# Rotary's swapped rows in the first block: twelve SBUF to SBUF DMAs per layer in place of sixteen permutation products

## The chip, the cores and the metric

One core of a Trainium2 chip runs the whole program in one launch. Its engines have a queue each: PE (TensorE, matrix products into PSUM, which has 8 banks), DVE (VectorE), ACT (ScalarE), POOL (GpSimd), and SP, which here only issues DMAs. They run beside each other and meet at semaphores. The metric is the time of one execution on the device in microseconds (us).

## The reference, cut to what matters

Two blocks of two layers each on 512 tokens of width 1024. The change is in the first block, in the rotary step of both of its layers. Of one layer:

```
h = x @ w_in[l]
c_q, c_kv, k_r, gate_a, q_d, k_d, v_d, gate_b, gates = split(h)
q_a = (rms_norm(c_q, g_q) @ w_q_up).reshape(8 heads, 64 + 32)
q_a = concat(q_a[..., :64], rotary(q_a[..., 64:], 32))
kv  = (rms_norm(c_kv, g_kv) @ w_kv_up)          # 8 heads, 64 (keys) + 64 (values)
k_a = concat(kv[..., :64], rotary(k_r, 32) for every head)
q_b, k_b = rotary(q_d, 16), rotary(k_d, 16)     # 4 heads x 2 halves of 64, first 16 of each
o_a = attention(q_a, k_a, v_a); o_b = differential_attention(q_b, k_b, v_d, lambda)
... gates, two branch products, merge, w_out, layer norm

rotary: x1, x2 = xr[:half], xr[half:]
        out = concat(x1 * cos - x2 * sin, x2 * cos + x1 * sin)
```

The second block (modulation, two feed-forward parts, a state space mixer) is not touched. It needs a vector `mod = silu(c) @ mod_w`, 9216 columns per layer, and the first block computes that beside its own work.

## The kernel before

Activations lie turned: channels on the 128 partitions, 512 tokens along the row. Each fp32 weight block of 128 x 1024 is fetched by SP into one of four slots (`w_raw`, line 136), copied by ACT into a high part (`w_hi`, L144), and POOL makes the low part (`w_lo`, L152). PE then makes three products per 128 x 128 piece (L158 to L160). SP fetches block n only when `w_lo` of block n - 4 is done, ACT makes `w_hi` of n only when PE has used block n - 4.

Work stands in an order written out by hand, the same in both layers. By blocks of the ring: 0 to 3 the latents and the rope key; 4 to 7 `QD`; 8 to 11 `KD`; 12 and 13 the heads of `QT` (banks `qh`), 14 the keys of all heads (`kh`, into `KTr`), 15 the values (`VA`); 16 to 19 the values `VD` (`values`, L178 to L180, which first waits for all four of its banks, and these are the banks that ACT's copies of `VA` free); 20 to 23 gate a; then the attention, with the rest of the weights as filler.

Rotary: the rows of a half are needed at the places of the other half. PE does this with a permutation matrix that also carries the sign (`rot_a`, `rot_d`, in `tables_sb`), in fp32, one product per head: four for `QD` between the products of `KD` (`swap`, L605), four for `KD` behind block 12, four for the heads 0 to 3 of `QT` behind block 13, and four for heads 4 to 7 between the key products. The result stands in banks 4 to 7. DVE then does three operations per head (`rotate`, L1044 to L1047): swapped rows times the sine table into `tmp`, x times cosine, and the sum. Sixteen heads in that order, `s_rot` counts them. The rope key is done the same way with one more product of its own (L616).

Behind the sixteen rotations, DVE works through `mod_w` in chunks of 128 x 1024 (`chunk`, L1086 and L1088, two operations each); 20 of them stand between the rotations and the attention, in groups of four. A group's four chunks add up in one of two sums (`macc_a`), and PE turns each sum by eight small products (`mod_turn`, L599), the first of them behind the third block of `VD`. A chunk is loaded by SP into one of five slots (L507). The first three chunks (0, 1, 2) stand in SP's queue at block 18, the next behind the fetch of block 24.

ACT's order there: copies of `QD`, `KD`, the rope key into all heads, `QT` heads 0 to 3, `w_hi` of 16, `QT` heads 4 to 7, `w_hi` of 17, eight copies of `KTr`, four of `VA`, `w_hi` of 18 and 19, and then `w_hi` of 20, which waits for the first block of `VD`.

## Time and profile before

| | us |
|---|---|
| median of 3 runs | 3594.82 |
| lowest, highest | 3591.64, 3597.8 |
| the profiled execution, own time | 3595.13 |
| its span in the trace | 3593.3 |
| PE busy | 3365.8 (94%) |
| PE weight load busy | 2630.1 (73%) |
| DVE busy | 2024.1 (56%) |
| ACT busy | 1170.8 (33%) |
| POOL busy | 1336.6 (37%) |

The span is what the trace covers; 1.83 us of the execution's own time lie around it. A product of 128 x 512 shows as about 0.39 us long, yet the next one starts 0.23 us after it: the ends are modelled and overlap, so PE's real pace is read from the starts. Busy shares are means over the whole program, while the change lies in two stretches of some 90 us, about 80 to 190 us and 622 to 732 us into the span. Where an engine stood idle, the row says in brackets for how long and what ended the wait.

### The profile page before, as it was taken

To read this page: it belongs to the slowest core of one execution; us is meant where nothing else is said; L and a number is where in the kernel's file an instruction comes from. 1 tells how busy PE (TensorE), PEld (TensorE's weight loads), DVE (VectorE), ACT (ScalarE), POOL (GpSimd) and SP (SyncE) were. 2 spreads that over 40 slices of the span, in tenths; PEclk is the share of its full clock that TensorE was granted. 3 is DMA by queue.
4 is the path that set the end of the run, shared out by engine and by line. 5 is a ranking of instruction groups with operands and counts; after the bars stand their busy time and mean duration, and the time that the engine had idled before them with its cause. 6 is when DMAs were issued, how large, how long until landed. Compare 5 with 4: busy or idle time off the path is not lost. (4 is left out here: it accounts for less than half of the span.)

```text
span 3593.3 us, 44542 instructions
## 1 busy us (share of the span) xinstructions
PE 3365.8 (94%) x16330; PEld 2630.1 (73%) x16330; DVE 2024.1 (56%) x2706; ACT 1170.8 (33%) x1792; POOL 1336.6 (37%) x565
## 2 busy tenths in 40 slices
PE   8999899999896999899998999969998999999997
PEld 6656677656675888787776888758887876778886
DVE  3876685876685444896274543154459944644412
ACT  3354323354323223333243222332233324332232
POOL 3302243302331445544043445534454521534453
PEclk9999999999997999999799999979999988999999
DMA  4513382513372332577123332233234951423321
GB/s 129 180 36 115 116 252 74 175 45 115 107 239 58 106 98 81 100 106 112 45 89 88 94 99 81 66 99 94 86 90 84 123 86 48 126 71 99 93 84 63
DMA packets 587729, 363.85 MB, mean 101 GB/s; under 512 B 57890, under 2 KB 537516, under 8 KB 587308
## 3 DMA queue, kind: packets, MB, share of 16 engines
q1 hardware_dynamic: 587188, 361.51, 38.7%
q8 instruction: 106, 1.74, 0.2%
q14 instruction: 59, 0.48, 0.0%
q10 hardware_dynamic: 376, 0.12, 0.0%
HBM read 346.63 MB, written 12.58 MB: 100 GB/s over the span
## 5 line engine op out<-in xcount | busy, mean ns | idle before, releaser
L152 POOL TENSOR_TENSOR w_lo<-w_raw,w_hi 128x1024 fp32r<-128x1024 f32 (+2 forms) x552 | 1328.6, 2412 | 2209.9 <-ACT w_hi L144 2209.6
L158 PE MATMUL bank<-xh,w_lo 128*128 128x512 f32 x2432 | 985.4, 405 | 61.2 <-DVE xl L2298 25.1
L160 PE MATMUL bank<-xh,w_hi 128*128 128x512 f32 x2432 | 971.8, 400 | 0.0
L159 PE MATMUL bank<-xl,w_hi 128*128 128x512 f32 x2432 | 971.2, 399 | 0.0
L144 ACT ACTIVATE w_hi<-w_raw 128x1024 fp32r<-128x1024 f32 (+2 forms) x552 | 564.8, 1027 | 787.4 <-PE bank L160 722.2
L158 PEld LDWEIGHTS bank<-xh,w_lo 128*128 128x128 f32 x2432 | 468.7, 193 | 185.6 <-issue 41.3
L159 PEld LDWEIGHTS bank<-xl,w_hi 128*128 128x128 f32 x2432 | 469.2, 193 | 106.0 <-issue 4.3
L160 PEld LDWEIGHTS bank<-xh,w_hi 128*128 128x128 f32 x2432 | 468.0, 192 | 101.4
L158 PE MATMUL bank<-HH,w_lo 128*128 128x512 f32 x704 | 278.6, 396 | 0.0
L160 PE MATMUL bank<-HH,w_hi 128*128 128x512 f32 x704 | 278.5, 396 | 0.0
L159 PE MATMUL bank<-HL,w_hi 128*128 128x512 f32 x704 | 278.4, 395 | 0.0
L2455 DVE SCALAR_TENSOR_TENSOR HL<-th,HH 128x512 f32 x88 | 244.0, 2773 | 10.9
L2451 DVE TENSOR_TENSOR th<-th,bank 128x512 f32<-128x512 f32 x88 | 60.5, 687 | 321.5 <-PE bank L160 320.4
L1088 DVE SCALAR_TENSOR_TENSOR macc_b_l<-m_raw_l,cs_l,macc_b_l 128x512 f32<-128x512 f32 x182 | 180.3, 991 | 6.9 <-DMA m_raw_l<-in_mod_w_dram 1.8
L2052 ACT ACTIVATE th<-bank 128x512 f32<-128x512 f32 x88 | 52.6, 598 | 392.9 <-PE bank L160 363.3
L2448 DVE SCALAR_TENSOR_TENSOR th<-th,bank 128x512 f32<-128x512 f32 x88 | 60.5, 687 | 180.2 <-ACT th L2052 180.2
L2271 DVE TENSOR_TENSOR tot_sq<-tot_sq,sqt 128x512 f32<-128x512 f32 x24 | 52.6, 2194 | 192.7 <-ACT sqt L2012 192.3
L158 PEld LDWEIGHTS bank<-HH,w_lo 128*128 128x128 f32 x704 | 132.2, 188 | 32.1
L160 PEld LDWEIGHTS bank<-HH,w_hi 128*128 128x128 f32 x704 | 132.2, 188 | 32.0
L159 PEld LDWEIGHTS bank<-HL,w_hi 128*128 128x128 f32 x704 | 132.2, 188 | 31.9
L2615 DVE TENSOR_REDUCE nm<-bank 128x1 f32<-128x128 f32 (+3 forms) x64 | 28.4, 486 | 175.3 <-PE bank L1916 175.3
L2260 DVE TENSOR_TENSOR ycr<-y,xT 128x512 f32<-128x512 f32 x30 | 31.3, 1045 | 126.5 <-ACT y L2009 126.2
(502 smaller groups left out, 4547.1 us busy)
## 6 DMA issues: line engine op xcount, KB each, us to landing
w_raw<-in_ffn_w_in_dram SPq DMA_DIRECT2D x176, 512.0 KB, 3.8
m_raw_l<-in_mod_w_dram SPq DMA_DIRECT2D x144, 512.0 KB, 5.1
w_raw<-in_w_in_dram SPq DMA_DIRECT2D x80, 512.0 KB, 4.0
w_raw<-in_mix_w_in_dram SPq DMA_DIRECT2D x64, 512.0 KB, 9.2
w_raw<-in_ffn_w_out_dram SPq DMA_DIRECT2D x64, 384.0 KB, 3.5
w_raw<-in_ffn_w_out_dram SPq DMA_DIRECT2D x64, 320.0 KB, 3.2
w_raw<-in_w_out_dram SPq DMA_DIRECT2D x16, 512.0 KB, 4.7
w_raw<-in_glu_w_dram SPq DMA_DIRECT2D x32, 256.0 KB, 3.1
```

What stands on the lines that cost most here:

```text
L144: nc.scalar.activation(ring.hi[s][:, 0:width], ring.raw[s][:, 0:width], ACT.Copy).then_inc(ring.hi_done, 1)
L152: nc.gpsimd.tensor_tensor(ring.lo[s][:, 0:width], ring.raw[s][:, 0:width], ring.hi[s][:, 0:width].bitcast(F32), ALU.subtract).then_inc(rin ...
L158: nc.tensor.matmul(out, wl, xh, start=start, stop=False)
L159: nc.tensor.matmul(out, wh, xl, start=False, stop=False)
L160: return nc.tensor.matmul(out, wh, xh, start=False, stop=stop)
L1088: ins = V.scalar_tensor_tensor(macc[:, :], w, cc, macc[:, :], ALU.mult, ALU.add)
L2052: nc.scalar.activation(th[v][:, :], bank[2 * v], ACT.Tanh, scale=0.5).then_inc(s["tanh"], 1)
L2260: V.tensor_tensor(to[:, :], y[:, m, :], xT[:, m, :], MUL).then_inc(s["y_cross"], 1)
L2271: V.tensor_tensor(tot["sq"][:, :], tot["sq"][:, :], sqt[m % 2][:, :], ADD).then_inc(s["y_added"], 1)
L2448: V.scalar_tensor_tensor(t[:, :], t[:, :], 1.0, bank[2 * v], ADD, MUL).then_inc(evac[2 * v], 1)
L2451: V.tensor_tensor(t[:, :], t[:, :], bank[2 * v + 1], MUL).then_inc(evac[2 * v + 1], 1)
L2455: V.scalar_tensor_tensor(HL[:, to, :], t[:, None, :], 0.5, HH[:, to, :].bitcast(F32), MUL, SUB).then_inc(s["hidden"], 1)
```

## The change

The sign of rotary moves from the permutation matrix into the sine table (the table's first half becomes negative, the matrix is 1 in both places), and the sixteen permutation products of `swap` are gone. In their place SP copies rows from SBUF to SBUF into two new tiles, `turned[0]` over `VA` and `turned[1]` over `PTr1`: four DMAs of 8 partitions x 8 KB (64 KB) for `QD`, four for `KD`, and two of 16 partitions x 8 KB (128 KB) for each half of `QT`'s heads. That is twelve per layer, each set under one semaphore that DVE waits for as a whole. DVE's first operation now reads `turned` in SBUF in place of a PSUM bank, and takes 80 of the 128 partitions for `QD` and `KD`. The rope key keeps its product.

POOL clears the partitions 0 to 63 of both tiles once per layer, behind `s_sums` 1 and ahead of block 8. As `turned[0]` lies over `VA`, ACT waits for the twelfth rotation before it copies `VA`. As `turned[1]` lies over a chunk slot, that slot (2) is used last of the five and its first load waits for the sixteenth rotation; only the chunks 0 and 1 are still loaded at block 18, and chunk 2 is loaded behind the fetch of block 24.

```diff
@@ -77,8 +77,9 @@
-            s[o + i] = s[o + half + i] = np.sin(ang[i].astype(np.float64))
-            r[o + half + i, o + i] = -1.0
+            s[o + half + i] = np.sin(ang[i].astype(np.float64))
+            s[o + i] = -s[o + half + i]
+            r[o + half + i, o + i] = 1.0
...
@@ -257,6 +258,7 @@
+    turned = [mem(f"turned{i}", [P, 4, T], F32, over=x) for i, x in enumerate(("VA", "PTr1"))]
...
@@ -343,11 +346,11 @@
-    slot_of = [i % 5 for i in range(FIRST_CH)] + [5 + i % 3 for i in range(24)] + [3 + i % 5 for i in range(28)]
+    slot_of = [(0, 1, 3, 4, 2)[i % 5] for i in range(FIRST_CH)] + [5 + i % 3 for i in range(24)] + [3 + i % 5 for i in range(28)]
...
-        first = B_VD + 2 if before[i] < 0 and i < 3 else B_VD + 9 if before[i] < 0 and i < FIRST_CH else B_GB + 8
+        first = B_VD + 2 if before[i] < 0 and i < 2 else B_VD + 9 if before[i] < 0 and i < FIRST_CH else B_GB + 8
...
@@ -493,11 +489,12 @@
-            elif i < 3:
+            elif i < 2:
                 sp.wait_ge(s_cn, 3)
-                sp.wait_ge(s_sums, 1)
             elif i < FIRST_CH:
                 sp.wait_ge(ring.used, B_VD)
+                if slot == 2:
+                    sp.wait_ge(s_rot, 16)
...
@@ -506,6 +503,16 @@
+        def swap_rows(i, x, heads, places, label):
+
+            wait_read(sp, label)
+            if i < 2:
+                sp.wait_ge(s_cleared, i + 1)
+            h = slice(heads[0], heads[-1] + 1)
+            for at, half in places:
+                for a, b in ((at, at + half), (at + half, at)):
+                    sp.dma_start(turned[i % 2][a:a + half, :, :], x[b:b + half, h, :]).then_inc(s_swapped[i], 16)
...
@@ -529,6 +536,16 @@
+            if n == 2 * RING + 8:
+                swap_rows(0, QD, range(0, HD), ((0, ROT // 2), (DH, ROT // 2)), ("qd", HD - 1))
+            if n == 3 * RING + 8:
+                swap_rows(1, KD, range(0, HD), ((0, ROT // 2), (DH, ROT // 2)), ("kd", HD - 1))
+            if n == 3 * RING + 9:
+                sp.wait_ge(s_rot, 4)
+                swap_rows(2, QT, range(0, 4), ((NOPE, ROPE // 2),), ("qh", 3))
+            if n == 3 * RING + 10:
+                sp.wait_ge(s_rot, 8)
+                swap_rows(3, QT, range(4, 8), ((NOPE, ROPE // 2),), ("qh", 7))
...
@@ -547,6 +564,10 @@
+            if n == 2 * RING:
+                pool.wait_ge(s_sums, 1)
+                for x in turned:
+                    nc.gpsimd.memset(x[0:DH, :, :], 0.0).then_inc(s_cleared, 1)
...
@@ -599,11 +620,6 @@
-        def swap(i, src, rot, rows=slice(0, P)):
-
-            out = free(pe, ("r", i))
-            nc.tensor.matmul(out[rows, :], rot[rows, rows], src, start=True, stop=True).then_inc(s_rotated, 1)
...
@@ -878,6 +882,7 @@
             copy(KTr[0:NOPE, h, :], ("kh", h), held(("kh", h))[0:NOPE, :])
+        act.wait_ge(s_rot, 12)
         for t in range(TT):
...
@@ -1062,12 +1067,19 @@
+        def rotate_rows(x, swapped, r, cos, sin):
+
+            step.mark(V.tensor_tensor(tmp[r, :], swapped, sin[r, :], ALU.mult))
+            step.done(dve, V.tensor_tensor(x, x, cos[r, :], ALU.mult))
+            return V.tensor_tensor(x, x, tmp[r, :], ALU.add)
...
         for i in range(16):
-            dve.wait_ge(s_rotated, i + 1)
+            dve.wait_ge(s_swapped[i // 4], 16 * (4 if i < 8 else 2))
```

SP's queue in the first layer, from the fetch of block 15 to that of block 21. Before (a name with the bracket is the semaphore waited for):

```order
L136 DMA w_raw_55<-in_w_kv_up_dram 128x8x64 [waits w_lo_done_l0]
L136 DMA w_raw_52<-in_w_in_dram 128x2x512 [waits w_lo_done_l0]
L136 DMA w_raw_53<-in_w_in_dram 128x2x512 [waits w_lo_done_l0]
L507 DMA m_raw_l_132<-in_mod_w_dram 128x2x512 [waits sums_l0,latent_split_l0]
L507 DMA m_raw_l_133<-in_mod_w_dram 128x2x512 [waits sums_l0,latent_split_l0]
L507 DMA m_raw_l_134<-in_mod_w_dram 128x2x512 [waits sums_l0,latent_split_l0]
L136 DMA w_raw_54<-in_w_in_dram 128x2x512 [waits w_lo_done_l0]
L136 DMA w_raw_55<-in_w_in_dram 128x2x512 [waits w_lo_done_l0]
L136 DMA w_raw_52<-in_w_in_dram 128x8x128 [waits w_lo_done_l0]
L136 DMA w_raw_53<-in_w_in_dram 128x8x128 [waits w_lo_done_l0]
```

And the same place now, from the second chunk load on:

```order
L504 DMA m_raw_l_135<-in_mod_w_dram 128x2x512 [waits latent_split_l0]
L137 DMA w_raw_54<-in_w_in_dram 128x2x512 [waits w_lo_done_l0]
L137 DMA w_raw_55<-in_w_in_dram 128x2x512 [waits w_lo_done_l0]
L515 DMA turned_l_105<-KD_l_88 8x2048 [waits turned_cleared_l0,evacuated3_l0]
L515 DMA turned_l_105<-KD_l_88 8x2048 x3
L137 DMA w_raw_52<-in_w_in_dram 128x8x128 [waits w_lo_done_l0]
L515 DMA turned_l_104<-QT_l_83 16x2048 [waits evacuated3_l0,rotary_ready_l0]
L515 DMA turned_l_104<-QT_l_83 16x2048
L137 DMA w_raw_53<-in_w_in_dram 128x8x128 [waits w_lo_done_l0]
L515 DMA turned_l_105<-QT_l_83 16x2048 [waits evacuated3_l0,rotary_ready_l0]
L515 DMA turned_l_105<-QT_l_83 16x2048
```

The copies of `KD` stand behind the fetch of block 19, those of `QT` behind the fetches of blocks 20 and 21; those of `QD` stand behind the fetch of block 15, and the third early chunk load is gone.

ACT's queue in the first layer, at the copies of the keys and of `VA` (`rotary_ready` is `s_rot`). Before:

```order
L843 ACTIVATE KTr_l_84<-bank 64x512 [waits latent_up_l0] x7
L843 ACTIVATE KTr_l_84<-bank 64x512 [waits w_used_l0]
L843 ACTIVATE VA_l_85<-bank 128x512 [waits latent_up_l0] x3
L843 ACTIVATE VA_l_85<-bank 128x512 [waits w_used_l0]
L144 ACTIVATE w_hi_58<-w_raw_54 128x1024 [waits w_used_l0,w_load2_l0]
L144 ACTIVATE w_hi_59<-w_raw_55 128x1024 [waits w_used_l0,w_load3_l0]
```

Now:

```order
L847 ACTIVATE KTr_l_84<-bank 64x512 [waits latent_up_l0] x7
L847 ACTIVATE KTr_l_84<-bank 64x512 [waits w_used_l0]
L847 ACTIVATE VA_l_85<-bank 128x512 [waits latent_up_l0,rotary_ready_l0]
L847 ACTIVATE VA_l_85<-bank 128x512 [waits latent_up_l0] x2
L847 ACTIVATE VA_l_85<-bank 128x512 [waits w_used_l0]
L145 ACTIVATE w_hi_58<-w_raw_54 128x1024 [waits w_used_l0,w_load2_l0]
L145 ACTIVATE w_hi_59<-w_raw_55 128x1024 [waits w_used_l0,w_load3_l0]
```

The order is the same; the first copy of `VA`, and with it all that stands behind it on ACT, now waits for DVE's twelfth rotation.

## Rows read from the trace of the kernel before

**Rows 1.** Timeline of PE, first layer: start us, us, engine, line, op, tiles, count, idle before.

```profile
100.52 0.40 PE L160 MATMUL bank<-xh,w_hi 128*128 128x512 f32 x1
...
101.85 0.39 PE L159 MATMUL bank<-cnl_l,w_hi 128*96 128x512 f32 x1
...
106.93 0.39 PE L160 MATMUL bank<-cnh_l,w_hi 128*96 128x512 f32 x1
...
...
110.83 0.39 PE L159 MATMUL bank<-cnl_l,w_hi 128*96 128x512 f32 x1
...
115.91 0.40 PE L160 MATMUL bank<-cnh_l,w_hi 128*96 128x512 f32 x1
...
120.07 0.39 PE L159 MATMUL bank<-cnl_l,w_hi 128*64 128x512 f32 x1
...
122.36 0.40 PE L160 MATMUL bank<-cnh_l,w_hi 128*64 128x512 f32 x1
...
123.94 0.40 PE L159 MATMUL bank<-cnl_l,w_hi 128*64 128x512 f32 x1
124.17 0.40 PE L160 MATMUL bank<-cnh_l,w_hi 128*64 128x512 f32 x1
```

**Rows 2.** Timeline of PE: end of the latent values, end of the stage.

```profile
132.37 0.39 PE L659 MATMUL bank<-w_hi,cnh_l 128*128 128x512 f32 x1
133.64 0.47 PE L178 MATMUL bank<-w_hi,xl 128*128 128x512 f32 x1 [0.89 <-ACT VA_l L843]
...
190.12 1.84 PE L599 MATMUL bank<-ones,macc_a_l 128*128 128x1 f32 x8 [3.59 <-DVE macc_a_l L1088]
```

**Rows 3.** Timeline of DVE, first layer: rotations and the first weight chunks.

```profile
108.29 0.69 DVE L1044 TENSOR_TENSOR PX_l<-bank,rope_sb_l 128x512 f32<-128x512 f32 x1 [3.56 <-PE bank L605]
...
110.34 0.69 DVE L1044 TENSOR_TENSOR PX_l<-bank,rope_sb_l 128x512 f32<-128x512 f32 x1
110.95 2.58 DVE L1045 TENSOR_TENSOR KD_l<-KD_l,rope_sb_l 128x512 f32<-128x512 f32 x1
...
119.71 2.79 DVE L1047 TENSOR_TENSOR QT_l<-QT_l,PX_l 32x512 f32<-32x512 f32 x1
...
128.65 0.69 DVE L1044 TENSOR_TENSOR PX_l<-bank,rope_sb_l 32x512 f32<-32x512 f32 x1
...
140.38 0.48 DVE L1086 TENSOR_SCALAR macc_a_l<-m_raw_l,cs_l 128x512 f32<-128x512 f32 x1
...
148.76 1.65 DVE L1088 SCALAR_TENSOR_TENSOR macc_a_l<-m_raw_l,cs_l,macc_a_l 128x512 f32<-128x512 f32 x2 [1.94 <-DMA m_raw_l<-in_mod_w_dram]
```

**Rows 4.** Timeline of POOL, first layer: the splits of weight blocks 15 to 17.

```profile
102.15 1.30 POOL L152 TENSOR_TENSOR w_lo<-w_raw,w_hi 128x512 fp32r<-128x512 f32 x1 [5.08 <-ACT w_hi L144]
110.57 2.41 POOL L152 TENSOR_TENSOR w_lo<-w_raw,w_hi 128x1024 fp32r<-128x1024 f32 x1 [7.12 <-ACT w_hi L144]
119.41 2.54 POOL L152 TENSOR_TENSOR w_lo<-w_raw,w_hi 128x1024 fp32r<-128x1024 f32 x1 [6.43 <-ACT w_hi L144]
```

**Rows 5.** Timeline of ACT: the evacuation of VA.

```profile
130.73 2.66 ACT L843 ACTIVATE VA_l<-bank 128x512 f32<-128x512 f32 x4
```

**Rows 6.** Timeline of SP: the chunk loads behind the fetch of block 24.

```profile
143.56 2.27 SPq L507 DMA_DIRECT2D m_raw_l<-in_mod_w_dram  x4
```

**Rows 7.** One line, L1635: small SBUF to SBUF DMAs, 8 to 64 KB each.

```profile
L1635 SPq DMA_DIRECT2D Mt<-Kn x64: 593/602/3148, 1644.2 to 2908.5; - x64
...
DMA to landing us min/median/max: 2.0/3.1/7.3
```

**Rows 8.** The page, DMA issues: KB each, median us to landing.

```profile
w_raw<-in_w_in_dram SPq DMA_DIRECT2D x80, 512.0 KB, 4.0
```

**Rows 9.** Timeline of PE, start of the second layer, after a wait.

```profile
564.00 0.76 PE L158 MATMUL bank<-xh,w_lo 128*128 128x512 f32 x1 [3.27 <-DVE xl L1290]
...
569.11 0.40 PE L158 MATMUL bank<-xh,w_lo 128*128 128x512 f32 x1
```

**Rows 10.** Table by stretches: PE, PEld, DVE, ACT, POOL busy, clock, DMA share, GB/s.

```profile
55.50:60.20 4.70, 4.70 (x12) 3.68 (x12) 4.39 (x7) 1.63 (x4) 2.74 (x1) 0.50 0.02 3
```

More of the change, by code:

```diff
@@ L290, in first_block @@
     s_sq, s_sums, s_std, s_cn = sem("squares"), sem("sums"), sem("std_ready"), sem("latent_split")
-    s_rotated, s_rot, s_kr, s_krb = sem("swapped"), sem("rotary_ready"), sem("k_rope"), sem("k_rope_spread")
+    s_rot, s_kr, s_krb = sem("rotary_ready"), sem("k_rope"), sem("k_rope_spread")
+    s_swapped, s_cleared = [sem(f"swapped{i}") for i in range(4)], sem("turned_cleared")
     s_th = sem("tanh_ready")
@@ L378, in first_block @@
         hold(("kd", s), s)
-        hold(("r", s), 4 + s)
     for s in range(4):
@@ L382, in first_block @@
     for s in range(4):
-        hold(("r", 4 + s), 4 + s)
-    for s in range(4):
         hold(("qh", 4 + s), s)
-    for s in range(4):
-        hold(("r", 8 + s), 4 + s)
     for s in range(HA):
         hold(("kh", s), s % 4)
-    for s in range(4):
-        hold(("r", 12 + s), 4 + s)
     for q in ("va", "vd", "ga"):
@@ L624, in _ @@
             product(free(pe, ("kd", s)), n, s, KT, xh, xl).then_inc(ring.used, 1)
-            wait_read(pe, ("qd", s))
-            swap(s, QD[:, s, :], rot_d)
         for b in range(2):
@@ L636, in _ @@
             last.then_inc(ring.used, 1)
-            for s in range(4):
-                if b == 0:
-                    wait_read(pe, ("kd", s))
-                    swap(4 + s, KD[:, s, :], rot_d)
-                else:
-                    wait_read(pe, ("qh", s))
-                    swap(8 + s, QT[NOPE:QK, s, :], rot_a, slice(NOPE, QK))
         wh, wl = weights(B_UP + 2, 2)
@@ L646, in _ @@
         for h in range(HA):
-            if h >= 4:
-                wait_read(pe, ("qh", h))
-                swap(8 + h, QT[NOPE:QK, h, :], rot_a, slice(NOPE, QK))
             c = slice(h * NOPE, (h + 1) * NOPE)
@@ L1047, in rotate @@
             return V.tensor_tensor(x, x, tmp[r, :], ALU.add)
-        rope, every = slice(NOPE, QK), slice(0, P)
+        rope = slice(NOPE, QK)
         dve.wait_ge(s_rope, 16)
```

5 lines of the change are left out of this document (3 added, 2 removed).

## The prediction

> **What bounds the kernel now.** I began with the page: PE is busy 94% of the span, so work taken from PE looks like time won. But the change lies in one stretch of each layer, so I read that stretch in the timelines of PE, DVE, ACT and SP, and asked which wait ends last there. PE sets the pace up to the values `VA`; its products start every 0.23 us (123.94, 124.17) [rows 1]. The end of the stretch is not PE's: PE has done its part of the first scores, and then stands 3.59 us until DVE has finished the twentieth chunk [rows 2]. DVE's own chain there has hardly a gap. It starts with the rotations of `KD` at 108.29, runs through all sixteen heads to the first chunk at 140.38, and waits 1.94 us at 148.76 for chunk 3, whose load SP issued behind the fetch of block 24 [rows 3, 6]. So two things set the end: when DVE is through its rotations, and when the first block of `VD` is used, since ACT's and POOL's splits, the fetch of block 24 and all later chunk loads hang on that. The reader is to see that a product taken from PE counts only as far as these two move.
>
> **What goes.** A swap's price is the distance between the products around it, less two steps of 0.23. For `QD` 101.85 - 100.52 - 0.46 = 0.87; the four of `KD` 110.83 - 106.93 - 0.46 = 3.44; the first four of `QT` 120.07 - 115.91 - 0.46 = 3.70; one of the last four 123.94 - 122.36 - 0.46 = 1.12 [rows 1]. Per layer 4 x 0.87 + 3.44 + 3.70 + 4 x 1.12 = 15.1 us, in two layers 30.2 us of PE. The last product of `VA` started at 132.37 [rows 2]; it moves to about 117.5, or 119.5 with some 2 us of waits for banks that the swaps covered before (estimate: two groups of ACT's copies, 0.6 each, and their start).
>
> **When the swapped rows of `KD` arrive.** The DMAs for `KD` stand behind the fetch of block 19, which waits for the low part of block 15. That was done at 102.15 + 1.30 = 103.45 [rows 4]. Three swaps stood before it on PE, so now 103.45 - 2.6 = 100.85. The fetch and four more issues at 0.57 to 0.59 each (the rate of the chunk loads and of L1635) put the last one at about 103.2 [rows 6, 7]. The trace has SBUF to SBUF copies of this size: from issue to landing 2.0 at least, 3.1 in the middle, 7.3 at most [rows 7]. So they land between 105.2 and 110.5. I take 107.0: the fetch in front of them lands 4.0 us after its issue [rows 8], at 104.9, and the shortest copy takes 2.0 more; the middle one gives 106.3.
>
> Two pages of the Trainium skill bear on this. "DMA: Bandwidth & Descriptors" (section on the anatomy of one DMA) has 2 us plus bytes over 436 GB/s, 2.15 us for 64 KB; the row's 3.1 is longer. By 2.15 the landing would be 105.4 and the sum 3.2 us lower. "SBUF — State Buffer" (Door 1: the DMA port swizzle) says that what counts is how many of the 16 ports the partitions reach, at 27.2 GB/s each. Eight partitions reach two ports, so, by that rule, a 64 KB copy moves for 1.2 us and four in line for 4.8; behind the fetch that is a landing at about 110, near my upper end. No row here shows a copy of 8 partitions.
>
> **The rotations.** Before, eight of them took from 108.29 to 128.65, 20.4 us: 2.05 each (108.29 to 110.34), and two stalls, 2.58 and 2.79 in place of some 0.7, each beside a split on POOL (110.57 and 119.41) [rows 3, 4]. Reading the first operand from SBUF costs the same: an operation on SBUF alone and one on PSUM differ by about 0.02, save that one more operation of each rotation can now be caught by POOL: a stall grows by 0.6 at most, or goes entirely (2 us) where the split falls into no rotation. The splits follow PE's products, which come 3.5 and 6 us earlier there (the swaps of rows 1 ahead of each, less the bank waits): about 107.0 and 113.2. With rows at 107.0 both still fall into the eight rotations: the twelfth rotation (four `KD`, four `QT`) is done at 107.0 + 20.4 = 127.4, only 1.2 us earlier than the 128.65 of before, though PE is far ahead. With rows at 105.2 it is 125.6; at 110.5 the first split is past, and it is 110.5 + 16.3 + 2.1 = 128.9. The copies of `QT` are issued behind the fetch of block 20 at about 110, and land by 116; `QD`'s rows land before 90, and its rotations end before 100. Neither is late.
>
> **The new wait on ACT.** The copies of `VA` wait for that twelfth rotation. Behind them on ACT stand `w_hi` of 18 and 19, and PE's `VD` waits for all four copies. From their start to the first product of `VD` it was 133.64 - 130.73 = 2.91 [rows 2, 5]. So `VD` starts at 127.4 + 2.9 = 130.3, 3.3 us earlier than before. Of the 13 us that PE is earlier at this point it stands and waits about 11.
>
> **What the wait costs beyond itself.** Behind a wait of 3.27 us at 564.00 the granted clock was low: twelve products took 569.11 - 564.00 = 5.11 in place of 2.75, so 2.36 us are lost [rows 9]. The page's other such stretch shows a granted clock of 0.50 at 55.5 to 60.2, which is 1.2 GHz of 2.4, with twelve products in 4.7 us [rows 10]. Behind 0.89 us at 133.64 nothing was lost [rows 2]. A wait of 11 us is on the side of the first. I take the whole 2.4 us; the bounds are 0 and some 3.
>
> **The chunks.** Chunk 3 was at work 148.76 - 133.64 = 15.1 us after `VD`'s start [rows 2, 3]; that is the load's chain through the first block of `VD`, the splits and the fetch. Chunk 2 now takes that place, and one chunk, 1.65 us, comes in between [rows 3]. The early part (chunks 0 and 1) is done before and hides. So chunk 3 starts at 130.3 + 2.4 + 15.1 + 1.7 = 149.5, where it was 148.76: 0.7 us later. From there on everything is as before: DVE, the loads and PE's first `mod_turn`, which now waits for chunk 3, shift together, and PE's 3.59 us before the scores become longer. POOL's two clearings lie at 54 to 58, where block 8's split may slip by 0.5 us; PE wants it 18 us later. SP's wait for `s_rot` 8 holds only block 22's fetch, and nothing needs that soon: no cost.
>
> Sum: +0.7 per layer, +1.4 for both. The profiled execution took 3595.13 (span 3593.3 and 1.83 around it), so 3596.5; the median of the runs shown is 3594.82, 0.3 lower, and I don't correct for that.
>
> **Rivals.** Two changes are told apart if they differ by over 0.2%, 7.2 us.
>
> (a) *PE is the bound after all.* Then the 30.2 us of products come back: 3565. For it speaks the 94%, against it the 3.59 us for which PE stands at the end of the stretch [rows 2], and the new wait on ACT. Even if all else shrank, DVE's chunks need the load behind `VD`. 5%.
>
> (b) *Early and warm.* The rows of `KD` land at 105.2 and the clock isn't lowered behind the wait: per layer 0.7 - 1.8 - 2.4 = -3.5, in all -7.0: 3588. For it speaks that a granted clock is the chip's choice; against it the row behind a wait of 3.27 us, shorter than this one [rows 9]. Where one stall on POOL is missed too, it passes the bound: 16% in all, 10% beyond it.
>
> (c) *The four copies of a set go one after the other.* Eight partitions at a time give the engines little to do at once. At 3.1 us each from 101.3 the rows of `KD` land at 113.7. The twelfth rotation is then done at 113.7 + 16.3 + 2.1 = 132.1, 4.7 us later than in my sum, and both layers give +1.4 + 9.4 = 3606. The place is DVE's wait for `KD`'s set, and from a landing at about 112 on (with a stall in it) the result is slower beyond the bound. For it speaks the 7.3 us at most; against it the median of 3.1, of copies that were issued eight at a time. 24%. The page on SBUF, as told above, points this way, but by its figure only as far as about 3599, inside my own case.
>
> **Numbers.** Forecast 55%, rival (a) 5%, (b) 16%, (c) 24%. The range 3586 to 3606 holds (b) and most of (c) and leaves (a) out. Slower by over 0.2%: most of (c) and a little of my own case, 0.24. Faster: (a) and part of (b), 0.15. Within: 0.61.
>
> **What would show it.** PE's products at L605 are gone, yet DVE's idle time before its first `KD` rotation ends at a DMA. `KD`'s rows land at 105 to 110, ACT idles some 8 us before the first copy of `VA`, ended by DVE; PE idles 10 us or so before L178's successor, and the granted clock is 0.5 behind it. The first `mod_turn` waits 1 to 3 us for DVE. I am wrong if `VD` starts much before 128 or after 133, if no clock is lost there, or if DVE's chunks are not what ends PE's last wait before the scores.

## The result and the profile after

| | before | after |
|---|---|---|
| median, us | 3596.4 (6 runs) | 3614.19 (6 runs) |
| lowest, highest | 3591.64, 3599.49 | 3605.32, 3616.83 |
| profiled execution, own time (span) | 3595.13 (3593.3) | 3616.4 (3614.6) |
| ratio | | 1.0048, 95% interval 1.0035 to 1.006 |
| PE busy | 3365.8 (94%) | 3351.3 (93%) |

The kernel is 0.5% slower, some 18 us; the forecast was 3596.5, with 3606 as the upper end. In a second series (below) the ratio was 1.0034, 12 us. The sixteen swaps per layer are gone, and PE's busy time fell by 14.5 us. The time did not follow it. One of the six executions of both_pad, a kernel further down, took 18,138 us at full clock for a reason that no trace here shows; without it that kernel's median would be 3619.08 in place of 3619.1.

PE, timeline (start, us, engine, line, operation, tiles, idle before and what ended it), first layer. In this execution everything runs 1.1 to 1.2 us later than in the one of before from the loads of x on; that is to be taken off when these rows are held against [rows 2].

```profile
104.57 0.40 PE L161 MATMUL bank<-cnh_l,w_hi 128*96 128x512 f32 x1
105.74 0.44 PE L159 MATMUL bank<-cnh_l,w_lo 128*96 128x512 f32 x1 [0.77 <-ACT QT_l L847]
...
131.35 0.76 PE L179 MATMUL bank<-w_hi,xl 128*128 128x512 f32 x1 [10.57 <-ACT VA_l L847]
...
152.27 1.02 PE L620 MATMUL bank<-ones,macc_a_l 128*128 128x1 f32 x8 [1.54 <-DVE macc_a_l L1100]
...
153.81 0.63 PE L181 MATMUL bank<-w_hi,xh 128*128 128x512 f32 x1
154.24 0.63 PE L179 MATMUL bank<-w_hi,xl 128*128 128x512 f32 x1
...
193.38 1.02 PE L620 MATMUL bank<-ones,macc_a_l 128*128 128x1 f32 x8 [3.59 <-DVE macc_a_l L1100]
```

`VD` starts at 131.35 behind the wait of 10.57 us, against 133.64 [rows 2]. Without the start-up shift that is 130.2, and 130.3 was forecast. The first `mod_turn` now waits 1.54 us, and the products behind it start 0.43 us apart, where 0.23 us is the pace at full clock. Before, it stood here and waited for nothing:

```profile
150.56 1.02 PE L599 MATMUL bank<-ones,macc_a_l 128*128 128x1 f32 x8
```

The wait ahead of the scores is 3.59 us as before.

DVE, timeline of the same stretch, to be held against [rows 3]:

```profile
108.45 2.72 DVE L1072 TENSOR_TENSOR PX_l<-turned_l,rope_sb_l 80x512 f32<-80x512 f32 x1 [9.40 <-DMA turned_l<-KD_l]
...
115.18 2.90 DVE L1073 TENSOR_TENSOR KD_l<-KD_l,rope_sb_l 80x512 f32<-80x512 f32 x1
...
132.38 2.75 DVE L1074 TENSOR_TENSOR QT_l<-QT_l,PX_l 32x512 f32<-32x512 f32 x1
135.16 2.75 DVE L1072 TENSOR_TENSOR PX_l<-turned_l,rope_sb_l 32x512 f32<-32x512 f32 x1
...
141.30 2.50 DVE L1098 TENSOR_SCALAR macc_a_l<-m_raw_l,cs_l 128x512 f32<-128x512 f32 x1
...
149.01 3.11 DVE L1100 SCALAR_TENSOR_TENSOR macc_a_l<-m_raw_l,cs_l,macc_a_l 128x512 f32<-128x512 f32 x4 [2.84 <-DMA m_raw_l<-in_mod_w_dram]
```

DVE idles 9.4 us until `KD`'s copies have landed, and then has four operations of 2.7 to 2.9 us beside POOL's splits. Its first chunk starts at 141.30, with the shift off where it started before. The four operations at 149.01 are chunks 2 and 3, behind one wait for chunk 2's load.

ACT's timeline, for [rows 5]; SP's, for [rows 6], with the copies; and the copies' line (issue in ns, minimum, median, maximum):

```profile
129.03 2.07 ACT L847 ACTIVATE VA_l<-bank 128x512 f32<-128x512 f32 x4 [10.36 <-DVE QT_l L1074]
```

```profile
102.46 2.66 SPq L515 DMA_DIRECT2D turned_l<-KD_l  x4
...
143.96 2.15 SPq L504 DMA_DIRECT2D m_raw_l<-in_mod_w_dram  x4
```

```profile
L515 SPq DMA_DIRECT2D turned_l<-KD_l x8: 624/636/642, 102.5 to 651.1; - x8
...
DMA to landing us min/median/max: 3.1/4.0/5.0
```

The landing times of the last row are those of the eight copies of `QT` (128 KB), 4.0 us at the median, where [rows 7] had 3.1 for others; the view gives none for the 64 KB copies of `QD` and `KD`. For `KD` the rows show this: the four were issued from 102.46 to 105.12, and the set had landed by 108.45, when DVE started, 6.0 us after the first issue began and 3.3 after the last ended. With the shift off that is 107.3 (forecast 107.0). Of the Trainium skill, "DMA: Bandwidth & Descriptors" had 2.15 us for a 64 KB copy, by a fit for DMAs that GpSimd issues, where these are SP's; 2.15 us is shorter than the 3.3 us here. The estimate from the ports of "SBUF — State Buffer" had the set land near 110, too late.

The granted clock, by stretches (PE, PEld, DVE, ACT, POOL busy, clock, DMA share, GB/s), for [rows 10]:

```profile
131.30:136.60 5.30, 5.25 (x13) 4.16 (x14) 5.23 (x4) 1.68 (x2) 4.49 (x2) 0.51 0.15 30
152.20:157.00 4.80, 4.73 (x18) 3.93 (x19) 4.67 (x4) 0.00 (x0) 2.13 (x1) 0.64 1.10 351
265.70:270.00 4.30, 3.04 (x8) 1.23 (x8) 4.16 (x8) 0.66 (x2) 0.00 (x0) 0.56 0.65 230
```

Three stretches lie wholly or in part at half clock (the second row mixes the two levels). The first was forecast; the other two were not. The third lies where attention A gives way to D, some 115 us behind the end of the changed stretch.

How much later the same product starts in after than in before is the best measure of where time goes. The table gives it in us, at the time in the kernel before, for the whole kernels as profiled and for the two with the second block left out (before_first, after_first), by 9.1 us at the median:

| PE product near | 78 | 104 | 131 | 134 | 140 | 152 | 160 | 195 | 255 | 275 | 500 | 700 | 780 | 815 | 1100 |
|---|---|---|---|---|---|---|---|---|---|---|---|---|---|---|---|
| before to after | 1.1 | -2.4 | -12.0 | -2.3 | 0.1 | 1.8 | 3.3 | 3.3 | 3.7 | 6.5 | 6.4 | 7.2 | 7.5 | 10.2 | 10.6 |
| first block alone | -0.3 | -3.8 | -13.4 | -3.7 | -1.2 | 0.4 | 1.9 | 1.9 | 2.5 | 5.4 | 5.4 | 6.0 | 6.4 | 9.2 | 9.6 |

PE is 13 us ahead at 131 and has lost it all at 152. Then come two steps that were in no term: the clock behind `mod_turn`, 1.5 us, and the clock at the change of attention, 2.8 to 2.9 us (275), which comes again in layer 2 (815). The rest comes in steps of some 0.5 us, as between 195 and 255.

### The profile page after: what moved, and what is told of

Its sections match the earlier page's. It is cut to its first block and busy times, and to the rows that moved or that the text cites. A ratio compares the mean times of both kernels' runs of the same rounds, so it can differ in the third digit from the quotient of the medians.

```text
span 3614.6 us, 44384 instructions
## 1 busy us (share of the span) xinstructions
PE 3351.3 (93%) x16266; PEld 2630.8 (73%) x16266; DVE 2025.4 (56%) x2706; ACT 1169.7 (32%) x1792; POOL 1347.2 (37%) x569
```

## The experiments

Each was timed in five rounds against before. "Ratio" is to before, with its 95% interval.

**The same kernels again, and the first block alone.** before_again and after_again are the kernels as they are. In before_first and after_first the line `if SECOND:` is `if False:`, so the second block's layers are not computed.

> The kernel before, unchanged: what one more set of executions and one more profile of the same program differ by. Theory: the ratio to before lies within 0.2% of 1, and its profiled execution keeps the granted clock of 1.00 at the change from attention A to D of both layers (near 262 and 798 us), as the first profile of before did. Rival (the further losses seen after the changed stage are differences between executions, not of the change): the clock falls there in this profile too, or second-block stretches (near 1650, 1740, 2360 us) are slower by 2 to 3 us each than in the first profile.

> The changed kernel, unchanged. Theory: 1.0048 times before again (1.0035 to 1.006), and its profile again shows about +2.0 us per layer in the rotary stage (a 1.5 us wait of the first modulation turn and a second stretch of half clock behind it), about +2.4 us per layer at the change from attention A to D, +8 to +10 us at the start of the second block and +17 to +21 at the end. Rival: the losses outside the rotary stage belong to that one execution and are gone or elsewhere in this one.

> The kernel before with the second block left out (its two layers are not computed; the rows that the first block leaves are written out). With after_first it gives what the change costs in the first block alone. Expected time about 1140 us (the second block began at about 1124 us in the profile).

> The changed kernel with the second block left out in the same way. Theory (the change costs time in the first block, and a further part arises in the second block's unchanged code): 8 to 10 us over before_first, ratio about 1.008, so that 8 to 10 us of the 17.8 us are the second block's. Rival 1 (all of it is of the first block): 16 to 19 us over before_first. Rival 2 (the first block costs only the rotary stage's 2 us per layer): 3 to 5 us.

Measured: before_again 1.0008 (0.9999 to 1.0017); after_again 3606.88 us, 1.0034 (1.0021 to 1.0048); before_first 1131.96, after_first 1141.03 us. So 9.1 us arise in the first block, and 3 to 9 us in the second, whose source text is unchanged. The fall at the change of attention came in after, after_again and after_first, and in none of the three of before. The wait ahead of it is the same 2.86 us in both (PE's timelines, before_again, then after_again):

```profile
264.72 0.66 PE L684 MATMUL bank<-tables_sb,PX_l 128*128 128x128 f32 x4 [2.86 <-DVE PX_l L1149]
265.31 1.13 PE L731 MATMUL bank<-KD_l,QD_l 64*128 64x512 f32 x4
```

```profile
267.38 1.12 PE L688 MATMUL bank<-tables_sb,PX_l 128*128 128x128 f32 x4 [2.86 <-DVE PX_l L1161]
268.43 2.08 PE L735 MATMUL bank<-KD_l,QD_l 64*128 64x512 f32 x4
```

In after's own profile the second block goes from +7.8 to +21.3; much of that is of that execution, since after_again ended at +11.8, and before_again itself drifted by 2.8 us inside the second block and back.

**The chunk's slot alone: before_slots**

```diff
-    slot_of = [i % 5 for i in range(FIRST_CH)] + [5 + i % 3 for i in range(24)] + [3 + i % 5 for i in range(28)]
+    slot_of = [(0, 1, 3, 4, 2)[i % 5] for i in range(FIRST_CH)] + [5 + i % 3 for i in range(24)] + [3 + i % 5 for i in range(28)]
-        first = B_VD + 2 if before[i] < 0 and i < 3 else B_VD + 9 if before[i] < 0 and i < FIRST_CH else B_GB + 8
+        first = B_VD + 2 if before[i] < 0 and i < 2 else B_VD + 9 if before[i] < 0 and i < FIRST_CH else B_GB + 8
-            elif i < 3:
+            elif i < 2:
-                sp.wait_ge(s_sums, 1)
```

> The kernel before with only the change's order of the modulation slots: chunk 2 is loaded behind fetch 24 into slot 3 and no longer early into slot 2; the swaps stay products. Theory (the late chunk 2 delays VectorE's first four chunks, TensorE waits at the first modulation turn and the clock falls behind it): +1.5 to +3 us per layer at the end of the value products, +3 to +6 us in all; and if the fall of the clock at the change from attention A to D follows from the shift alone, another 2.9 us per layer, +9 to +12 us. Rival (the turn's wait comes from the late rotations and not from the chunk): under +1 us per layer and within 0.1% of before.

Measured: 3603.48 us, 1.0019 (1.001 to 1.0028). With every swap still a product, the late chunk 2 alone makes the first `mod_turn` wait and the clock fall behind it:

```profile
153.39 1.26 PE L598 MATMUL bank<-ones,macc_a_l 128*128 128x1 f32 x8 [1.37 <-DVE macc_a_l L1087]
154.51 0.77 PE L178 MATMUL bank<-w_hi,xl 128*128 128x512 f32 x1
155.08 0.63 PE L179 MATMUL bank<-w_lo,xh 128*128 128x512 f32 x1
```

PE stands 3.0 us later at 160 than at 147, and 2.9 us in the second layer. The clock at the change of attention fell in layer 2 alone. By its profile the first block ends as late as after's (+11.0 at 1100, 1.35 of it start-up; after +10.6 and 1.14). So the late chunk is enough for a loss of that size in the first block, without any of the DMAs, but it is made up otherwise: 3.0 and 2.9 us at the two turns and one fall at the change of attention, where after has 2.2 and 0.6 us in the stage and two such falls.

**Taking away the waits one at a time.** after_chunk2 gives chunk 2 its early load back, after_turn_later moves the first turn, after_vd_banks takes away the 10.6 us wait (the lines that matter; what only follows from them is left out):

```diff
 after_chunk2
+    turned += [turned[0], mem("turned3", [P, 2, 3 * T], F32, over="SG")]
-    slot_of = [(0, 1, 3, 4, 2)[i % 5] for i in range(FIRST_CH)] + [5 + i % 3 for i in range(24)] + [3 + i % 5 for i in range(28)]
+    slot_of = [i % 5 for i in range(FIRST_CH)] + [5 + i % 3 for i in range(24)] + [3 + i % 5 for i in range(28)]
...
+        first = B_VD + 6 if i == 2 else B_VD + 2 if before[i] < 0 and i < 2 else B_VD + 9 if before[i] < 0 and i < FIRST_CH else B_GB + 8
...
+            elif i == 2:
+                sp.wait_ge(s_rot, 8)
...
 after_turn_later
-    turned_after = [chunk_at[4 * g + 3] + 1 for g in range(NGR)]
+    turned_after = [chunk_at[4 * g + 3] + (2 if g == 0 else 1) for g in range(NGR)]
-    per = {B_VD: 2, B_VD + 1: 2, B_VD + 2: 2, B_VD + 3: 3, B_GA: 3, B_GA + 1: 3, B_GA + 2: 3, B_GA + 3: 2}
+    per = {B_VD: 2, B_VD + 1: 2, B_VD + 2: 2, B_VD + 3: 2, B_GA: 4, B_GA + 1: 3, B_GA + 2: 3, B_GA + 3: 2}
 after_vd_banks
-    for q in ("va", "vd", "ga"):
-            hold((q, s), s)
+    for q, b in (("va", 0), ("vd", 4), ("ga", 0)):
+            hold((q, s), b + s)
...
```

> The changed kernel with the swapped rows of QT's heads 4 to 7 in the part of SG that the query products have read, so that PTr1's slot comes free with rotation 8: chunk 2 is loaded before the fetch of block 22 and the order of the slots is that of before. The ScalarE wait for rotation 12 stays. Theory: the wait at the first modulation turn and the clock's fall behind it go (1.5 to 3 us per layer), the cold stretch at VD's start stays; 3 to 6 us under after. Rival (the late rotations alone are the cause of that wait): within 1 us of after.

> The changed kernel with the first modulation turn one value block later on TensorE (behind block 19 of the ring, not 18) and with VectorE's ninth chunk one block later, as the buffer needs it. Theory: the 1.5 us wait at the first turn and the second stretch at half clock behind it go, so that TensorE stands 1.5 to 3 us per layer earlier at 160 us than in after, 3 to 6 us in all, and more if the fall at the change of attention goes with it. Rival (VectorE's chunks set the end of the stage): the wait turns up at a later turn or at the scores and the time is that of after.

> The changed kernel with VD's four value products in banks 4 to 7 instead of 0 to 3 (and the first modulation turn in bank 0), so that TensorE does not wait for ScalarE's copies of VA, which wait for the twelfth rotation. Theory (VectorE's rotations and chunks set the stage): the 10.6 us wait at VD's start goes, but comes back as a wait at the first modulation turn (10 us or more there), with the turn's end and the start of the scores within 1 us of after's; time within 3 us of after, ratio to before 1.002 to 1.006. Rival (that wait and the cold clock behind it are the cost): 5 us or more per layer less than after, below the kernel before.

Measured: after_chunk2 3605.01 us, 1.0027 (1.0018 to 1.0036); after_turn_later 3602.81, 1.0015 (1.0006 to 1.0024); after_vd_banks 3610.63, 1.004 (1.0026 to 1.0054).

In after_chunk2 the turn waits 0.63 us, and the clock does not fall behind it:

```profile
151.47 1.02 PE L626 MATMUL bank<-ones,macc_a_l 128*128 128x1 f32 x8 [0.63 <-DVE macc_a_l L1106]
152.36 0.48 PE L179 MATMUL bank<-w_hi,xl 128*128 128x512 f32 x1
152.68 0.39 PE L180 MATMUL bank<-w_lo,xh 128*128 128x512 f32 x1
```

Its first block ended level with before's (+1.3 us at 1100, before_again +1.9). Its total is 9 us over before all the same, and 4.2 us of that come in one place of the second block, to which I come below. after_turn_later brought PE to 160 us 4 us earlier than after, and to the end of the first block 7 us (start-up off), more than the forecast 1.5 to 3 per layer; both falls at the change of attention stayed. after_vd_banks shows where the 10.6 us go when nothing waits for ACT: to the turn.

```profile
149.00 1.84 PE L622 MATMUL bank<-ones,macc_a_l 128*128 128x1 f32 x8 [11.69 <-DVE macc_a_l L1102]
```

**The second block: code that stands elsewhere.** In all six profiles of kernels with PE's shorter program (after, after_again, after_chunk2, after_turn_later, after_vd_banks, after_shift) PE stops at one place in the second block's first pass, for 2.4 to 3.1 us, and waits for nothing the profile shows (after's PE timeline):

```profile
1654.79 1.51 PE L1907 MATMUL bank<-U,Bti 128*64 128x64 f32 x45
1659.19 1.01 PE L1907 MATMUL bank<-U,Bti 128*64 128x64 f32 x13 [2.89 <-issue]
```

The DMA view of after for 1654 to 1660 (queue: packets, MB, share of 16 engines) has a block of instructions arriving just there, beside a busy data queue; it had none from 1650 to 1654, where the data queue's share was 100.2%:

```profile
q1 hardware_dynamic: 1268, 0.56, 66.2%
q8 instruction: 1, 0.02, 2.0%
```

The Trainium skill, "Runtime: NRT & Kernel Launch", section on instruction fetch mechanics, says that each engine's instructions are refilled in 16 KiB blocks of 256 through a DMA queue of its own while the previous ones run, and that crossing a block's end is mostly hidden. The row's 0.02 MB agrees in size; that it is hidden does not hold here. To test it, 20 one-element products per layer bring PE's program back to its length (18,564 instructions; before 18,566, after 18,406):

```diff
+        moved = free(pe, "moved")
+        for _ in range(20):
+            nc.tensor.matmul(moved[0:1, 0:1], ones[0:1, 0, 0:1], ones[0:1, 0, 0:1], start=True, stop=True)
         pe.wait_ge(s_root, 3 + HD)
-        packed_spread(nc, free(pe, "moved"), lmean[:, :], ident).then_inc(s_spread, 1)
+        packed_spread(nc, moved, lmean[:, :], ident).then_inc(s_spread, 1)
```

> The changed kernel with 20 products of one element each (1x1, a result that nothing reads) at the end of TensorE's part of the first block in each layer, where it waits for the layer's last roots: they bring back the number of instructions that the 32 removed swaps took from TensorE's program (18,564 of 18,566; after has 18,406), so that the second block's code stands where it stood. In every profile of a kernel without the swaps so far TensorE stands 2.4 to 3.1 us at L1895 of the second block's first pass waiting for nothing that the profile shows, and in none of the kernels with them. Theory (a stall in the supply of TensorE's instructions that depends on where the code stands): that stall is gone and the time is 3 to 5 us under after. Rival (it comes from something else in the change, its DMAs or the shift in time): the stall is there as before and the time is that of after.

> The kernel before with the same 20 one-element products per layer at the same place, so that the second block's TensorE code stands 158 instructions further on with the same work and the same DMAs. Theory (code position alone moves stalls about): the first block is unchanged to 1 us; in the second block a stall of 2 to 3 us may appear at another place, or none. Rival (the products themselves cost or hide something): 1 us or more is lost or won at the end of the first block's layers, where they stand.

> after_chunk2 with the 20 one-element products per layer of after_pad. after_chunk2's first block ended 0.5 us under before_again's and its second block cost 7 us more, 4.2 us of it at L1895. Theory (chunk order and the clock's falls in the first block, code position in the second): 3 to 5 us under after_chunk2, within 0.15% of before. Rival (the second block's loss comes from the change itself): as after_chunk2, 1.0027.

Measured: after_pad 3613.23 us, 1.0044 (1.0031 to 1.0057); before_pad 1.0005 (0.9996 to 1.0013); chunk2_pad 3603.04, 1.0016 (1.0001 to 1.0032). The stall is gone in every padded kernel, the three below included. chunk2_pad's PE timeline at the place:

```profile
1647.58 2.04 PE L1916 MATMUL bank<-U,Bti 128*64 128x64 f32 x64
1649.54 0.51 PE L159 MATMUL bank<-xh,w_lo 128*128 128x512 f32 x1
```

So the traces show that the stall goes with the place of the code. That it is the supply of instructions is argued from the block that arrives there. The time doesn't show it: after_pad has a ratio like after's, not the 3 to 5 us less that were expected. Between 1640 and 1660 it lost nothing, where after_again lost 2.9 us, but between 500 and 700 us it lost 7.5 us where after lost 0.8 (the first turn of layer 2 waited 4.26 us), and one profile can't say how often that happens. chunk2_pad is 2 us under after_chunk2 by the medians, with intervals that overlap. before_pad's profile has no stall, but its first block did not stay within the 1 us that was expected: the clock was at half from 120.3 us on for 6.6 us, in the first layer, where the program is still that of before and PE waited for nothing. PE was 1.2 us later than in before at 115 us and 4.4 at 125. So a fall that costs 3 us can come in one execution and stay away in others of the same first layer.

**No wait on ACT: both_pad.** chunk2_pad, and (in part)

```diff
-    turned += [turned[0], mem("turned3", [P, 2, 3 * T], F32, over="SG")]
+    turned += [mem("turned2", [P, 4, T], F32, over="SG", skip=4096 * 3), mem("turned3", [P, 2, 3 * T], F32, over="SG")]
-        act.wait_ge(s_rot, 12)
+        act.wait_ge(s_rot, 4)
```

> chunk2_pad, and QT's first four heads' swapped rows in SG's last quarter, PX0 and PX1 in place of VA's room, so that ScalarE copies VA without waiting for rotation 12. TensorE then has no 10.6 us wait at VD's start and no cold clock there. Theory (VectorE's rotations and chunks set the end of this stage, and TensorE's wait only changes place): TensorE stands about 12 us earlier at VD's start, waits about as long at the first modulation turn or at the first gate products, and is at most 1 us per layer earlier than chunk2_pad at the first scores; the time is within 2 us of chunk2_pad's. Rival (ScalarE's wait costs): 5 us per layer or more under chunk2_pad, and faster than before.

Measured: 3619.1 us, 1.0063 (1.005 to 1.0076), 16 us over chunk2_pad. The wait moved as expected, and grew:

```profile
149.73 1.84 PE L626 MATMUL bank<-ones,macc_a_l 128*128 128x1 f32 x8 [15.22 <-DVE macc_a_l L1109]
151.43 0.77 PE L179 MATMUL bank<-w_hi,xl 128*128 128x512 f32 x1
```

That it costs so much was in neither theory. POOL's timeline tells it, first of chunk2_pad, then of both_pad:

```profile
131.96 5.26 POOL L153 TENSOR_TENSOR w_lo<-w_raw,w_hi 128x1024 fp32r<-128x1024 f32 x2 [14.58 <-ACT w_hi L145]
```

```profile
118.25 5.50 POOL L153 TENSOR_TENSOR w_lo<-w_raw,w_hi 128x1024 fp32r<-128x1024 f32 x2 [4.91 <-ACT w_hi L145]
124.55 2.72 POOL L153 TENSOR_TENSOR w_lo<-w_raw,w_hi 128x1024 fp32r<-128x1024 f32 x1 [0.80 <-ACT w_hi L145]
130.15 2.56 POOL L153 TENSOR_TENSOR w_lo<-w_raw,w_hi 128x1024 fp32r<-128x1024 f32 x1 [2.88 <-ACT w_hi L145]
135.74 2.47 POOL L153 TENSOR_TENSOR w_lo<-w_raw,w_hi 128x1024 fp32r<-128x1024 f32 x1 [3.03 <-ACT w_hi L145]
```

PE no longer waits, so the splits of the next weights come early and fall between DVE's rotations. Each that does turns an operation of 0.7 us into one of 2.8. From 78 us to the first chunk DVE has eight such operations instead of five, and the first chunk starts at 143.59 instead of 141.15, though the rotations of `KD` began 4.0 us earlier (104.17 against 108.13). (after_vd_banks has eight as well, and 142.86.) The wait on ACT had kept POOL off DVE's back. That is the first part of the 16 us. The profiles have the rest as well: both_pad's clock also fell at both changes of attention (2.8 us each), and between 500 and 700 us it lost 6.9 us where chunk2_pad lost 0.5.

**What makes the clock fall at the change of attention: before_shift and after_shift**

```diff
             sp.dma_start(tables[:, :], big[:, :]).then_inc(s_tab, 16)
+            sp.wait_ge(s_tab, 16)
```

> The kernel before with SyncE waiting for the table's DMA before it issues the loads of x, so that everything behind is 2 to 4 us later and nothing else differs. Theory (the fall at the change from attention A to D follows from what TensorE did ahead of it, not from the time): the granted clock stays 1.00 there in both layers, as in four profiles of the kernel before with and without small changes, and the time is 2 to 4 us over before. Rival (it follows from the moment alone): the clock falls there in at least one layer, and the time is 5 to 10 us over before.

> The changed kernel with the same wait. Theory: the clock falls at the change of attention in both layers as in after, after_again and after_first, and the second cold stretch behind the first modulation turn is there as well; 2 to 4 us over after. Rival (the moment decides): one or both of the falls are gone, and the time is 0 to 4 us under after in spite of the later start. The stall of 2.4 to 3.1 us at the second block's L1895 is there by either, as TensorE's code stands where it does in after.

Measured: before_shift 3596.11 us, 1.0001 (0.9991 to 1.0011), no fall in either layer though PE ran 2.6 us later there; after_shift 3610.3, 1.0038 (1.0025 to 1.0051), both falls, and the stall in the second block. The table by stretches, before_shift, then after_shift:

```profile
262.00:275.00 13.00, 10.14 (x57) 7.00 (x58) 12.41 (x25) 4.93 (x12) 0.06 (x1) 1.00 0.41 123
```

```profile
262.00:275.00 13.00, 10.14 (x45) 6.16 (x42) 12.19 (x25) 3.38 (x9) 0.00 (x0) 0.74 0.39 121
```

So the time since the start doesn't decide it. The length of the wait doesn't either: it is 2.86 us everywhere. Nor does the kernel: pairs_slots_first and pairs_slots_pad (below) have the same first block, and in layer 1 the clock fell in the first alone. The stretch before and the stretch behind the fall, then the same wait in the second:

```profile
255.68:257.60 1.92, 0.00 (x0) 0.00 (x0) 1.85 (x6) 1.66 (x6) 0.00 (x0) 1.00 0.40 36
257.70:262.00 4.30, 3.46 (x9) 1.63 (x10) 4.17 (x8) 0.60 (x1) 0.00 (x0) 0.50 0.59 224
```

```profile
252.82:255.68 2.86, 0.00 (x1) 0.00 (x1) 2.75 (x8) 1.66 (x6) 0.00 (x0) 1.00 0.55 156
255.70:260.00 4.30, 4.30 (x20) 2.91 (x21) 4.13 (x9) 0.60 (x1) 0.00 (x0) 1.00 0.36 139
```

The fall comes inside the wait, 2.0 us after PE stopped, and not behind it.

What tells the two apart is in the traces' record of the granted clock. In each trace all changes of the clock lie on one even row of instants (to 0.003 us), so the instants at which nothing changed are known too. The wait comes in both layers of all twenty profiles, 40 times, and one instant lies inside it each time. In the 18 with a fall that instant came 1.9 to 2.4 us after PE had stopped, and the clock fell right there. In 21 without a fall it came after 1.1 to 1.8 us. The groups don't overlap, though their nearest two members are only 0.04 us apart. (In the fortieth, layer 1 of after_vd_banks, it came after 0.9 us; the clock fell at the next instant, behind the wait.) after has it 2.0 to 2.1 us into the wait, before 1.3 and 1.6.

So what a change does there is to move PE, by a few us or less, against these instants. The shift moved both: the instant lies 1.1 us into layer 1's wait in before_shift and 1.9 in after_shift, close to where it was, so these two runs could not show it. Why executions of one kernel come so near the same place is not shown, and these figures are of this one wait; they are no rule for others.

**Giving DVE its rows earlier: pairs_pad and pairs_slots_pad.** chunk2_pad, with `KD`'s copies in two groups of two heads, the first behind the second head (shown in part; the second group has a semaphore of its own); the second kernel also loads chunks 3 and 4 one fetch earlier. before_early is that load alone, in before. pairs_slots_first is pairs_slots_pad without the second block.

```diff
-            if n == 3 * RING + 8:
-                swap_rows(1, KD, range(0, HD), ((0, ROT // 2), (DH, ROT // 2)), ("kd", HD - 1))
+            if n in (3 * RING + 6, 3 * RING + 8):
+                k = 2 * (n > 3 * RING + 6)
+                swap_rows(1, KD, range(k, k + 2), ((0, ROT // 2), (DH, ROT // 2)), ("kd", k + 1))
 before_early (pairs_slots_pad: the same 9 to 8)
-        first = B_VD + 2 if before[i] < 0 and i < 3 else B_VD + 9 if before[i] < 0 and i < FIRST_CH else B_GB + 8
+        first = B_VD + 2 if before[i] < 0 and i < 3 else B_VD + 8 if before[i] < 0 and i < FIRST_CH else B_GB + 8
```

> chunk2_pad with KD's swapped rows moved in two groups of two heads (eight DMAs in place of four), the first behind KD's second head, so that VectorE can rotate heads 0 and 1 while it waited for all four (8.9 us idle in chunk2_pad). Theory (VectorE's rotations set the end of this stage once the copies are late): its first KD rotation starts at 97 to 102 us instead of 108.7, the first modulation chunk 2 to 5 us earlier than in chunk2_pad, TensorE's wait at VD's start falls from 10.5 us by as much, and the time is 2 to 8 us under chunk2_pad. Rival (the later copies of QT or the loads of the modulation chunks set it): the first chunk starts where it did, and the time is that of chunk2_pad within 1 us.

> pairs_pad, and the loads of chunks 3 and 4 issued before the fetch of block 24 rather than behind it. Theory: chunk 3 no longer waits for its load, TensorE has no wait at the first modulation turn and VectorE reaches the scores 1 to 3 us per layer earlier than in pairs_pad; 2 to 6 us under it, and under the kernel before. Rival (a load that the queue waits for holds up the fetches behind it): the fetch of block 24 comes late, TensorE waits for weights at VD's last block or the first gate product, and the time is that of pairs_pad or more.

> The kernel before with only the loads of chunks 3 and 4 issued before the fetch of block 24 rather than behind it. Theory (in the kernel before these loads still wait for the last latent product, at 131 us, and VectorE's rotations end at 140 us by TensorE's pace): the wait of 1.9 us for m_raw near 149 us goes, worth 0 to 2 us per layer, 0 to 4 us under before. Rival (the wait inside the queue delays the fetch of block 24): TensorE waits for weights at the first gate products, 1 to 4 us over before.

> pairs_slots_pad with the second block left out, as before_first does (1131.96 us) and after_first (1141.03 us). Theory (4.1 us per layer won in the rotary stage, as the profile of pairs_slots_pad shows, and the clock's fall at the change of attention in some executions, 2.8 us per layer): 1123 to 1129 us. Rival (the profiled execution was a favourable one and the stage wins nothing): 1131 to 1134 us.

Measured: pairs_pad 3594.01 us, 0.9999 (0.9987 to 1.001); pairs_slots_pad 3593.78, 0.9997 (0.9987 to 1.0008); before_early 1.0009 (0.9999 to 1.0019); pairs_slots_first 1129.43 (1125.25 to 1134.44) against 1131.96 (1128.77 to 1133.7) for before_first, between its theory and its rival. DVE's waits from 78 to 160 us (waiting tile, releaser: us in total, times, longest), chunk2_pad, then pairs_pad:

```profile
DVE PX_l L1081 <- DMA turned_l<-KD_l: 9.5, 1, 9.5
DVE PX_l L1081 <- DMA turned_l<-QD_l: 9.1, 1, 9.1
```

```profile
DVE PX_l L1082 <- DMA turned_l<-QD_l: 9.7, 1, 9.7
DVE PX_l L1082 <- DMA turned_l<-QT_l: 3.2, 1, 3.2
DVE PX_l L1082 <- DMA turned_l<-KD_l: 2.4, 1, 2.4
```

The first chunk starts at 137.76 instead of 141.15, and PE's wait at `VD` falls:

```profile
127.79 0.76 PE L179 MATMUL bank<-w_hi,xl 128*128 128x512 f32 x1 [6.58 <-ACT VA_l L857]
```

The loss of chunk2_pad is gone. The earlier chunk loads added nothing that can be told, in either kernel. No version beats the kernel before measurably: the best is 0.03% under it, inside its interval.

## Why the prediction was wrong

Its picture of the stage was right, and nearly to the numbers. The products were worth nothing (rival (a) is out): PE was 13 us ahead and stood 10.57 us. `KD`'s rows had landed by 107.3 (107.0), `VD` started at 130.2 (130.3), and 2.3 us of clock were lost behind the wait (2.36). That `VD` fits to 0.1 us is in part luck: ACT's first copy of `VA` began at 127.9, 0.5 us later than the 127.4 of the sum, and `VD` followed it after 2.3 us where the sum had 2.9. The first `mod_turn` came 1.7 us later as recorded, 0.6 with the shift off; my sum for the chunks was 0.7. Rival (c)'s serial copies did not happen: the set of `KD` had landed 6.0 us after its first issue, where four times 3.1 would be 12.4. The time of 3606 that it gave is nearer to the result than mine, by another cause.

The step that failed is the sentence behind the sum: "From there on everything is as before". Three things are not.

1. *The wait at the first turn.* I named it (1 to 3 us, it was 1.54) and priced it at nothing beyond the 0.7. Behind it the clock fell a second time, for 1.5 us. I had read "0.89 us cost nothing, 3.27 us cost 2.36" [rows 2, 9] and asked it of one wait only. before_slots makes the wait and the fall with the swaps in place; after_chunk2 brings the wait down to 0.63 us and has no fall. With it the stage costs 2.2 us in layer 1. In layer 2 it is 0.6 (5.4 at 500, 6.0 at 700 in the table).
2. *The change of attention.* 2.9 us per layer, the largest part of the first block's 9.1, in a place that I never looked at. Before, PE waits 2.86 us there and keeps full clock. after, after_again, after_first, after_shift and after_pad lose it in each layer; before, before_again, before_first, before_shift, before_pad and before_early in none. What decides is where the wait lies against the instants at which the granted clock changes. The change moved it; before_slots, with another shift, had the fall in layer 2 alone, and one first block had it in one execution and not in another. So it is a cost of this change by where it happens to put PE, and not of the copies.
3. *The second block.* 3 to 9 us. One part is shown in the traces: a stall of 2.4 to 3.1 us in all six profiles with the shorter program, gone in all five with the old length restored. The times do not confirm it (after_pad is no faster than after), and what makes up the rest is open; it moves from execution to execution.

The forecast of 61% for "no change" was too sure: the range was built from terms of one stage, and had nothing for the other 3500 us.

## What to carry to other kernels

When work is taken from the engine that looks busiest, ask which other engine's chain ends the stage, and feed that one first: here the DMAs cost nothing only once DVE got its rows in two parts. A wait that is removed lets everything behind it come earlier, also what then collides (POOL's splits with DVE's rotations); a wait may be what keeps them apart. And price each new wait of 1 to 3 us on PE twice, for itself and for the clock behind it, and look for waits of that size far behind the change that have cost nothing so far: a shift of PE can turn each of them into a loss, or a loss into nothing.

## What was unexpected of the hardware

- The same wait of 2.86 us kept full clock 21 times and lost it 18 times; the difference is 2.8 to 2.9 us. The clock fell where one of the instants of its record lay 1.9 to 2.4 us behind PE's stop, and not where it lay 1.1 to 1.8 us behind it.
- In before_pad the clock was at half for 6.6 us from 120.3 us on though PE waited for nothing; in the profiles of before, whose text is the same up to there, that stretch ran at full clock.
- With 160 of 18,566 instructions out of PE's program PE stopped for 2.4 to 3.1 us near 1655 us, in code that had not changed; putting 158 back ended it.
- Issuing a copy of 8 partitions (64 KB) took 0.64 us of SP's queue, one of 16 partitions (128 KB) 0.57 us at the median (507 to 598 ns); the latter landed 3.1 to 5.0 us after the issue, and the four of `KD` had landed 3.3 us after the last issue ended.
